# Block attention: the first four of eight pairs' softmax weights turned by VectorE and a DMA exchange instead of TensorE, their outputs one to two steps later

## The reference, cut to what matters

```python
q, k, v = jnp.split(h @ w_in, 3, axis=-1)
q = partial_rope(to_heads(q), cos, sin)
k = partial_rope(to_heads(k), cos, sin)
v = to_heads(v)
...
s_own = jnp.einsum('bhqd,bhkd->bhqk', q_c, k_own).astype(jnp.float32) * scale
s_own = jnp.where(k_pos[None, :] <= q_pos[:, None], s_own, NEG_INF_2)
if n_sel == 0:
    p = jax.nn.softmax(s_own, axis=-1).astype(v.dtype)
    return jnp.einsum('bhqk,bhkd->bhqd', p, v_own)
...
return o.transpose(0, 2, 1, 3).reshape(B, S, H * hd) @ w_out
```

## Time and profile before

| | us |
|---|---|
| median of 3 runs | 1203.67 |
| lowest and highest | 1203.28, 1203.8 |
| the profiled execution, its whole time | 1204.34 |
| its span, first to last instruction | 1202.5 |
| TensorE busy | 1190.7 (99%) |
| VectorE busy | 951.1 (79%) |
| ScalarE busy | 622.3 (52%) |

### The profile page before, as it was taken

How to read it: one execution, slowest core, us unless ns; L and a number is a source line. 1 busy time by engine, 2 the same in 40 slices (tenths; PEclk the granted TensorE clock), 3 DMA queues, 4 the chain that set the end, 5 groups by cost and what they waited for, 6 DMA issues and landing times.

```text
span 1202.5 us, 14724 instructions
## 1 busy us (share of the span) xinstructions
PE 1190.7 (99%) x5734; PEld 976.3 (81%) x5734; DVE 951.1 (79%) x1382; ACT 622.3 (52%) x851; POOL 100.7 (8%) x153
## 2 busy tenths in 40 slices
PE   9999999999999999999999999999999999999997
PEld 7888888888778888888887778888887778888885
DVE  7799868977766689888786768898998888775656
ACT  7445346465774464334465657443446576643441
POOL 2110130221300010000000000000100000000000
PEclk9999999999999999999999999999999999999999
DMA  9999896874655489899467547888856764566640
GB/s 318 345 334 326 308 300 188 289 246 161 179 175 172 152 294 355 311 314 324 166 217 252 155 124 273 266 305 280 310 191 216 244 175 140 178 220 214 192 159 35
DMA packets 167830, 282.71 MB, mean 235 GB/s; under 512 B 23361, under 2 KB 97553, under 8 KB 167761
## 3 DMA queue, kind: packets, MB, share of 16 engines
q1 hardware_dynamic: 148368, 213.93, 53.7%
q0 software_dynamic: 19232, 67.77, 16.8%
q10 hardware_dynamic: 160, 0.07, 0.0%
HBM read 274.61 MB, written 7.13 MB: 234 GB/s over the span
## 4 chain that ended last, share of the span: by engine, by line
PE 89%; DVE 4%; ACT 3%; issue 2%; DMA 1%; SPq 0%; DVEq 0%
PE ps L549 23%; PE ps L551 22%; PE ps L550 22%; PE ps L882 7%; PE ps L881 3%; ACT hi_w L1205 2%; PE ps L801 2%; PE ps L749 1%; DVE lo_w L1721 1%; PE ps L628 1%; PE ps L755 1%; PE ps L1092 1%; PE ps L958 1%; DMA w_raw<-in_diff_w_in 1%; ACT area L1522 1%
## 5 line engine op out<-in xcount | busy, mean ns | idle before, releaser
L1721 DVE TENSOR_TENSOR lo_w<-w_raw,hi_w 128x2048 fp32r<-128x2048 f32 x194 | 440.8, 2286 | 66.0 <-ACT hi_w L1205 65.6
L1205 ACT ACTIVATE hi_w<-w_raw 128x2048 fp32r<-128x2048 f32 x195 | 370.2, 1916 | 60.5 <-DMA w_raw<-in_ffn_w_in 15.5
L549 PE MATMUL ps<-hi_w,xT 128*128 128x512 f32 x848 | 338.8, 400 | 0.0
L551 PE MATMUL ps<-lo_w,xT 128*128 128x512 f32 x848 | 331.0, 390 | 0.0
L550 PE MATMUL ps<-hi_w,xT 128*128 128x512 f32 x848 | 330.4, 390 | 0.0
L549 PEld LDWEIGHTS ps<-hi_w,xT 128*128 128x128 f32 x848 | 159.3, 188 | 36.6 <-issue 5.0
L549 PE MATMUL ps<-hi_w,hT_hi 128*128 128x512 f32 x480 | 188.3, 392 | 0.0
L551 PEld LDWEIGHTS ps<-lo_w,xT 128*128 128x128 f32 x848 | 159.2, 188 | 34.4
L551 PE MATMUL ps<-lo_w,hT_hi 128*128 128x512 f32 x480 | 187.0, 389 | 0.0
L550 PE MATMUL ps<-hi_w,hT_lo 128*128 128x512 f32 x480 | 186.8, 389 | 0.0
L550 PEld LDWEIGHTS ps<-hi_w,xT 128*128 128x128 f32 x848 | 159.5, 188 | 31.0
(11 more groups left out here) (324 smaller groups left out, 1153.3 us busy)
## 6 DMA issues: line engine op xcount, KB each, us to landing
w_raw<-in_ffn_w_in SPq DMA_DIRECT2D x86, 512.0 KB
aux<-in_ada_w POOLq DMA_DIRECT2D x34, 1024.0 KB, 6.9
w_raw<-in_mlp_w_up SPq DMA_DIRECT2D x32, 1024.0 KB
w_raw<-in_mlp_w_down SPq DMA_DIRECT2D x32, 1024.0 KB
w_raw<-in_w_mix_in SPq DMA_DIRECT2D x26, 1024.0 KB
w_raw<-in_ffn_w_out SPq DMA_DIRECT2D x22, 1024.0 KB
area<-in_ada_w POOLq DMA_DIRECT2D x14, 1024.0 KB, 6.0
w_raw<-in_moba_w_in SPq DMA_DIRECT2D x12, 1024.0 KB
```

The lines of the kernel that those rows point to most:

```text
L549: pe.matmul(dst, lhs_hi, rhs_hi, start=start, stop=False)
L551: return pe.matmul(dst, lhs_hi, rhs_lo, start=False, stop=stop)
L1205: act.activation(hi_w[:, ring_slot(u), :], w_raw[:, ring_slot(u), :], ACT.Copy).then_inc(w_hi, 1)
L1721: vec.tensor_tensor(lo_w[:, ring_slot(u), :], w_raw[:, ring_slot(u), :], hi_w[:, ring_slot(u), :].bitcast(F32), ALU.subtract).then_inc(w_l ...
```

## The change

For pairs 0 to 3 of the block attention TensorE no longer turns the weights (`W0` to `W3` are gone from the table), and ScalarE no longer copies them. In their place VectorE turns the 32x32 blocks of the 128x768 weights into `moba_probsT`, right behind `shares(c)`; SP writes them to DRAM with four transfers of 96 KB (`weights_save`), and when all four have landed reads them back with one transfer of 384 KB (`weights_load`), into three buffers. `moba_probsT` is the one source of the saves, so VectorE's turning of pair c waits until the save of pair c-1 has landed. SP's new transfers stand between the loads of units 12 to 16 of the stage and the exchange of the queries, which is split in two for it. TensorE's outputs move: `O0` from behind step 7 to behind step 8, `O1` from 8 to 9, `O2` from 9 to 10, `O3` from the middle of step 10 to the middle of step 11. Pairs 4 to 7 and the second attention (`diff`) keep their way.

```diff
-MOBA_SLOTS = ATTENTION + [(10, ["O3", "H3"], ["S4"]), (11, ["S5"], ["W4", "S6"]), (12, ["O4", "W5", "S7"], ["O5", "W6"]),
+MOBA_ATTENTION = ATTENTION[:6] + [(6, [], ["S1"]), (7, [], ["S2"]), (8, [], ["S3", "O0"]), (9, [], ["O1"])]
+P_SENT = 4
+MOBA_SLOTS = MOBA_ATTENTION + [(10, ["H3"], ["S4", "O2"]), (11, ["S5", "O3"], ["W4", "S6"]), (12, ["O4", "W5", "S7"], ["O5", "W6"]),
...
+        moba_sent = [part(9216, 768), aux[:, 3072:3840], part(8192, 768), part(9216, 768)]
...
+            def weights_save(c):
+                sp.wait_ge(p_turned, c + 1)
+                for a in range(4):
+                    rows = slice(32 * a, 32 * a + 32)
+                    sp.dma_start(p_dram[c].rearrange("y i k -> i y k")[:, :, rows],
+                                 moba_probsT[rows, :].rearrange("p (y j) -> p y j", j=32)).then_inc(p_saved, 16)
+
+            def weights_load(c):
+                sp.wait_ge(p_saved, 64 * (c + 1))
+                if c == 3:
+                    sp.wait_ge(at_o, NA_H + 1)
+                sp.dma_start(moba_sent[c].rearrange("p (x n) -> p x n", n=P),
+                             p_dram[c].rearrange("(x b) i n -> (b i) x n", b=4)).then_inc(p_landed, 16)
+
+            def weights_sent(u):
+                if 0 <= u - 13 < P_SENT - 1:
+                    weights_load(u - 13)
+                if 0 <= u - 12 < P_SENT:
+                    weights_save(u - 12)
...
                     if i == 2:
-                        late_heads(first + 1, 1)
+                        late_save(first + 1, 1)
+                    if not diff:
+                        weights_sent(2 * len(QKV_BLOCKS) + i)
+                    if i == 2:
+                        late_load(first + 1, 1)
+                if not diff:
+                    weights_load(P_SENT - 1)
...
                 def outputs(c):
-                    pe.wait_ge(at_p, ab + c + 1)
+                    if not diff and c < P_SENT:
+                        pe.wait_ge(p_landed, 16 * (c + 1))
+                        weights = moba_sent[c]
+                    else:
+                        pe.wait_ge(at_p, tb + c + 1)
+                        weights = moba_probsT
...
+                    elif not diff and 2 <= c < P_SENT + 2:
+                        vec.wait_ge(p_turned, c - 1)
                     elif not diff and c >= 2:
-                        vec.wait_ge(at_t, ab + c - 1)
+                        vec.wait_ge(at_t, tb + c - 1)
...
                     ins.then_inc(at_shares, 1)
+                    if c < P_SENT:
+                        vec.wait_ge(at_shares, c + 1)
+                        if c >= 1:
+                            vec.wait_ge(p_saved, 64 * c)
+                        vec.transpose(moba_probsT, probs[c % 2]).then_inc(p_turned, 1)
```

More of the change, by code:

```diff
@@ L241, in two_blocks_kernel @@
         head_dram = nc.dram_tensor("head_scratch", (8, 32, 32, P), F32, kind="Internal").ap()
+        p_dram = nc.dram_tensor("weights_scratch", (P_SENT, 24, 32, P), F32, kind="Internal").ap()
         mod_dram = nc.dram_tensor("mod_scratch", (96, P), F32, kind="Internal").ap()
@@ L461, in square, with late_save @@
                 unit(u, w[:, 4 * half:4 * half + 4, n * BANK:(n + 1) * BANK], 4)
-            def late_heads(n, half):
+            def late_save(n, half):
                 blocks = [head_dram[n].rearrange("y i k -> i y k")[:, :, 32 * a:32 * a + 32] for a in range(4)]
@@ L468, in late_heads, with late_load @@
                         .then_inc(late_saved, 16)
+            def late_load(n, half):
                 sp.wait_ge(late_saved, 64 * (n - 3))
@@ L471, in late_heads, with qkv_out @@
                              head_dram[n].rearrange("(x b) i n -> (b i) x n", b=4)).then_inc(late_landed, 16)
-            def qkv_out(u0, w_in, w_out, first):
+            def late_heads(n, half):
+                late_save(n, half)
+                late_load(n, half)
+            def weights_save(c):
[15 more added lines that the diff above has]
+                    weights_save(u - 12)
+            def qkv_out(u0, w_in, w_out, first, diff):
                 w_in = w_in.rearrange("(k p) n -> p k n", p=P)
@@ L520, in _ @@
             swiglu(U_FFN2, d["ffn2_w_in"][0], d["ffn2_w_out"][0])
-            qkv_out(U_MOBA, d["moba_w_in_2"][0], d["moba_w_out_2"][0], 4)
+            qkv_out(U_MOBA, d["moba_w_in_2"][0], d["moba_w_out_2"][0], 4, False)
             mlp(U_MLP1, 0)
-            qkv_out(U_DIFF, d["diff_w_in_2"][0], d["diff_w_out_2"][0], 6)
+            qkv_out(U_DIFF, d["diff_w_in_2"][0], d["diff_w_out_2"][0], 6, True)
             mlp(U_MLP2, 1)
@@ L1050, in attention @@
             def attention(s, u0, pb, hb, ab, ch_o, diff):
+                tb = ab - P_SENT
                 def heads_T(n):
@@ L1085, in weights_T @@
                         pe.wait_ge(at_shares, c + 1)
-                    pe.wait_ge(at_p, ab + c)
+                    pe.wait_ge(at_p, tb + c)
                     if c == 4 and not diff:
@@ L1104, in outputs @@
                             pe.matmul(ps[mine[e], off:off + SEQ], v2[:, 0, v_of[e]],
-                                      moba_probsT[:, e * 3 * P:e * 3 * P + SEQ], start=True, stop=False)
+                                      weights[:, e * 3 * P:e * 3 * P + SEQ], start=True, stop=False)
                         for e in range(2):
                             mm = pe.matmul(ps[mine[e], off + P:off + SEQ], v2[:, 1, v_of[e]],
-                                           moba_probsT[:, e * 3 * P + SEQ:(e + 1) * 3 * P], start=False, stop=True)
+                                           weights[:, e * 3 * P + SEQ:(e + 1) * 3 * P], start=False, stop=True)
                         mm.then_inc(at_o, 1)
@@ L1559, in weights_out @@
                 def weights_out(c):
-                    act.wait_ge(at_t, ab + c + 1)
+                    act.wait_ge(at_t, tb + c + 1)
+                    if not diff and c == P_SENT:
+                        act.wait_ge(p_saved, 64 * P_SENT)
                     act.wait_ge(at_o, ab + c)
@@ L1617, in attention @@
                 before = []
-                for slot, between, events in ATTENTION:
+                for slot, between, events in ATTENTION if diff else MOBA_ATTENTION:
                     if 2 <= slot and slot % 2 == 0:
@@ L1635, in attention @@
                 project_out(4)
-                weights_out(3)
-                taken(2)
+                if diff:
+                    weights_out(3)
+                taken(2 if diff else 1)
                 split_hi(u0 + 14)
                 last_heads_out()
-                taken(3)
+                if diff:
+                    taken(3)
                 exps(4)
@@ L1648, in attention @@
                 else:
+                    taken(2)
                     split_hi(u0 + 15)
+                    taken(3)
                     exps(5)
@@ L2582, in attention @@
                     before = events
-                outputs(2)
+                outputs(2 if diff else 1)
                 rotate(3)
                 split_lo(u0 + 14)
-                outputs(3)
                 if diff:
+                    outputs(3)
                     first_rstd()
@@ L2620, in attention @@
                     scores(4)
+                    outputs(2)
                     shares(4)
                     scores(5)
+                    outputs(3)
                     split_lo(u0 + 15)
```

3 lines of the change are left out of this document (2 added, 1 removed).

## The result

The changed kernel took 1210.28 us (median of 6 runs, 1207.78 to 1214.92), the kernel before beside it 1203.74 us (6 runs): a ratio of 1.0055 [1.0045, 1.0065], 6.5 us slower. Five more runs (the last experiment) gave 1208.89 us against 1203.53: 1.0047 [1.0033, 1.0060], 5.4 us slower. Forecast was +4.0 us.

A forecast was written before the change was run, and what follows sets the result against it. TensorE, busy 1190.7 of 1202.5 us, was taken as the bound. Profiled: 1204.34 - 2.52 removed + 6.5 of waits = 1208.3; median: 1203.67 + 4.0 = 1207.7 us, with 1204.8 to 1212.5 to hold 8 of 10.

The forecast's parts named there:

- What bounds, and the removed work: TensorE bounds the kernel; four weight turnings of 0.63 us leave its list, a gain of at most 2.5 us.
- VectorE's turnings: Block attention: each added turning takes 0.94 us, partly hidden in pauses; together rotate(3) ends +1.0 us later, at 679.5.
- The waits for saves: VectorE's turnings wait for the previous pair's save: turning 1 0.3 us, turning 2 none, turning 3 1.7 us.
- `H3` at 681.5: TensorE's turning of heads 3 in step 10 starts at 679.5 + 0.3 + 1.7 = 681.5, before it 679.09.
- The outputs: TensorE waits for loaded weights: O0 0 to 0.7 us, O1 3 to 5 hidden before H3, O2 none, O3 counted 0.
- The 6.5 us of waits in the sum: TensorE's added waits in the block attention: about 3.5 us at O1 and 3 us at H3.
- the change is (start of `H3` - 679.09) + 1.60 us: End of the kernel moves by H3's delay plus 1.60 us of outputs now behind it: +4.0 us.
- rival (D): TensorE's clock falls in the waits at O1 and H3: +4 + 5.7, 1213.4 us at most; chance 0.09.
- the likeliest case's own range: The forecast case, +2.5 to +7 us for the whole kernel, 1206.1 to 1210.7 us; chance 0.56.
- (A): No slower or faster: no waits, H3 starts before 677.5, down to -2.5 us, 1201.2 us; chance 0.12.
- (B): Exchanges quick at 5.0 us, only VectorE's +1.0 us counts: H3 at 679.5, +2.0 us, 1205.7 us; chance 0.15.
- (C): Each save takes 9.4 us; turnings 1 and 3 wait 2.8 and 6.9 us: +11.7 us, 1215.4 us; chance 0.08.

The follow-up runs named there:

- e6: e4 with the rotation of heads 3 done earlier, before the shares of pair 3; weights neither turned nor sent: 1201.62 us, 0.9986 of the kernel before.
- e4: Changed kernel without weight transfers, their waits and VectorE's four turnings; outputs 0 to 3 formed from x: 1203.35 us, 0.9997 of the kernel before.
- e12: The changed kernel run again, unaltered, with a new profile: 1208.89 us, 1.0047 of the kernel before.
- e3: Changed kernel without weight saves, loads and their waits; VectorE still turns, outputs 0 to 3 formed from x: 1207.43 us, 1.0027 of the kernel before.
- e1: Changed kernel with the weights passing through unused places of the heads' DRAM scratch, no new tensor: 1208.94 us, 1.0039 of the kernel before.
- e10: e9 with TensorE running four sets of throwaway products ahead of its wait for output 1's weights: 1207.88 us, 1.0032 of the kernel before.
- e11: Changed kernel with two buffers for turned weights, earlier rotation of heads 3, and outputs 1 to 3 re-placed: 1208.52 us, 1.0034 of the kernel before.
- e7: Changed kernel with two buffers for turned weights, so a turning waits for the save of the pair before the last: 1207.85 us, 1.0035 of the kernel before.
- e9: e7 with output 3 moved half a step later, ScalarE's and VectorE's work for it moved to match: 1208.63 us, 1.0036 of the kernel before.
- e8: Changed kernel with only the rotation of heads 3 done earlier, as in e6: 1207.94 us, 1.0037 of the kernel before.

## Why the prediction was right, and where its sum was short

**What bounds, and the removed work: right.** The four turnings leave, and e6 shows that they are worth 2.0 us, of 2.52 forecast, once nothing else holds TensorE. e4 shows that without such a move they are worth 0.4 us, which isn't clear of no change.

**VectorE's turnings: right.** A turning takes 0.98 us (0.94 taken). From VectorE's division for pair 0 to the end of `rotate(3)` it took 678.51 - 650.51 = 28.00 us before, and 28.78 us in e12, with its waits for saves taken off: +0.8 us, where +1.0 was forecast. e3, with turnings and no transfers, has `H3` at 679.42 (679.5 forecast).

**The waits for saves: right in place, short in size.** Turning 1 was to wait 0.3 us, turning 2 not, turning 3 1.7 us, 2.0 us in all. Measured 0.94, 0 and 1.87 us in e12, 0.57, 0 and 2.38 us in the first profile: 2.8 and 2.95 us. From the first issue to the landing of a whole save it took, in e12, 659.15 - 651.86 = 7.3 us for pair 0 and 676.48 - 670.77 = 5.7 us for pair 2, within the 5.0 to 9.4 us assumed.

**`H3` at 681.5: right, the last tenths by luck.** 681.66, 681.39 and 681.43 us in the three profiles. The waits for saves were 0.8 us longer than forecast in e12, and VectorE reached the division for pair 0 at 649.79, 0.7 us earlier than before (650.51), which the forecast didn't have. The two cancel. Why VectorE is earlier there is open.

**The outputs: right.** `O0` found its weights, `O1` waited 2.9 us (3 to 5 forecast, so just under), `O2` and `O3` didn't wait, and the wait of `O1` is hidden under that of `H3`: e1 and e12 differ by the clock between the two, not by the start of `H3`. The 6.5 us of waits in the sum were 2.94 + 1.85 = 4.79 us in e12, and slow products between them took the rest: 5.40 us from `O1` to where TensorE stands at `H3` (679.58), in place of 3.75.

**The step that was short: "the change is (start of `H3` - 679.09) + 1.60 us".** It supposes that TensorE works at full speed behind `H3`. It doesn't: `H3` to `S4` takes 5.40 us in e12 in place of 3.77, +1.63 us. This is rival (D), which had 0.09 as something apart with up to 5.7 us. It is no case apart but a term of the forecast's own case, put at nothing in its sum: e3 and e10 show that the waits which this sum counts are what brings the lower clock. Two of the prediction's own signs say so. `S4` starts 3.97 us later than 682.86, not 2 to 3, and TensorE's clock leaves 1.00 in these steps (0.66 to 0.70), which stood under "Wrong". The first median still fell into the likeliest case's own range (1206.1 to 1210.7 us), near its upper end, with a term that this case didn't hold. For e12 the sum becomes 681.43 - 679.09 + 1.60 = 3.94, and 1.63 for the clock: 5.57 us. Output 7 stands 714.75 - 709.14 = 5.61 us later. The span is 5.1 us longer. The 0.5 us between are given back in the second attention: 0.2 us by its third scores (952.52 before, 957.88 in e12) and 0.3 us by its `H3` (972.38 and 977.44), where the kernel before waited 0.26 us for VectorE's rotation and e12 doesn't wait. So TensorE did have a later pause in which a delay could be given back, which the prediction denied.

The question that the prediction left open is answered by the runs: two waits with products between them are enough. The granted clock was 0.66 behind the first and 0.69 (0.70 in e12) behind the second. That agrees with the section of the Trainium skill cited there ("TensorE: Matmul & The Clock Gate", "HAM oscillation — how this bites in real kernels"), by which TensorE's waits for transfers bring the lower clock. In e3 a wait for VectorE did the same (0.70), and in e1 a wait of 2.82 us for a transfer did not (1.00).

The Trainium skill's other section ("VectorE: DVE Perf Modes", "The three transpose paths") gives its factor of 19 for a large innermost stride at the destination. The estimate of hundreds of us from it isn't borne out for these exchanges, in which DMA moves runs of 32 numbers after a turning inside 32x32 blocks: saves 0 and 2, of six squares each, took 7.3 and 5.7 us. A plain DMA turning of single elements wasn't run.

**The rest of the first median** (1210.28 against 1208.89 us) goes with runs that scatter up to 1214.92. The one profiled among them had 5.16 us of delay before the block attention. The other runs have no profile, so this is likely, and not shown for each.

**The other rivals.** (A) needed `H3` before 677.5. e4 and e6, without turnings and exchanges, have that (676.8 and 674.7), and their medians are below zero, by 0.4 us (within the interval of no change) and by 2.0 us; e11 has it too (674.0) and is slower all the same, for what it then meets at `S4`. (B) is e3's `H3`, and would have been +2.0 us at full clock. (C) needed saves of 9.4 us each; only the saves of pairs 1 and 3 came near (9.9 us from 660.23 to a load that also waited its turn on SP, and 8.7 us), and no turning of VectorE waited for these.

## What to carry to other kernels

TensorE's work taken away is gained only if what TensorE meets next is ready that much sooner; here VectorE's rotation was 0.6 us ahead, and each mended wait uncovered the next, from `H3` to `O1`, `O3` and `S4`. Where a sum contains a wait of TensorE of about 3 us, price the lower clock behind it as a term of the sum and not as a rival apart: here it cost 1.4 to 2.9 us where it came in the block attention, and of eleven waits of 2.8 to 3.9 us it failed to come behind two. And an exchange added beside another one shares its engines: their share in 660 to 675 us rose from 0.62 to 1.09 in e12, and the queries' read back took 6.3 us in place of 4.1.

## What the runs showed of the hardware

- Waits of TensorE and the lowest clock granted behind them, in 5 us stretches: 3.87 us (e3): 0.70; 3.71 (e7): 0.68; 3.42 (e9): 0.50; 3.39 (e1, at `H3`): 0.78; 3.29 (e8): 0.66; 3.19 (e11): 0.50; 3.02 (first profile, near 250 us): 0.66; 2.94 (e12): 0.66; 2.88 (first profile): 0.66. But 3.37 (e11, near 250 us): 1.00; 2.82 (e1, at `O1`): 1.00; 1.73 and 1.62 (e4): 1.00. Nearly the same wait can bring it or not, and it can cost 1.4 us (e7) or 2.6 us (e9: 6.32 us for 3.75 us of work).
- At the lower clock consecutive products of 128x512 start 0.43 us apart, and 0.23 us at full clock.
- Work whose result is thrown away kept the clock up: 2.8 us of it ahead of `O1` brought `H3` forward by 1.94 us (e10 against e9).
- VectorE's turning inside blocks takes 0.98 us for 128x768 and 1.25 us for 128x1024.
- The four issues of a save of weights took SP 3.2 to 7.1 us with other transfers ahead of them; those of the queries took 3.1 us on an idle queue.
